# Two-block transformer kernel: post-norm sums of squares added on VectorE, and both scan directions' scores in one block

## The reference

```
scores = einsum('bhtd,bhjd,bhtjd->bhtj', qi, ki, decay)      # j <= t forward, j >= t backward
o_intra = einsum('bhtj,bhje->bhte', scores, vi)
o = rms_norm(o_f + rev(o_b), gn) * silu(cg)
```

```
x = x + rms_norm_2(mix, mix_post_g[l])
x = x + rms_norm_2(memory_cross_attention(...), mem_post_g[l])
x = x + rms_norm_2(conv_ffn_2(...), ffn_post_g[l])
```

## Time and profile before

| | |
|---|---|
| Median of 3 runs | 3217.31 us (3217.26 to 3220.99) |
| The profiled execution: time | 3217.78 us |
| The profiled execution: span from the first to the last instruction | 3216.0 us |
| Mean granted TensorE clock | 0.963 of full speed |
| TensorE matmuls busy | 2983.4 us, 93% |
| VectorE busy | 1520.6 us, 47% |
| ScalarE busy | 1281.8 us, 40% |
| GpSimd busy | 327.6 us, 10% |
| DMA | 254.09 MB, 79 GB/s in the mean |

### The profile page before, as it was taken

How to read it: one execution, slowest core, us unless ns; L and a number is a source line. 1 busy time by engine, 2 the same in 40 slices (tenths; PEclk the granted TensorE clock), 3 DMA queues, 4 the chain that set the end, 5 groups by cost and what they waited for, 6 DMA issues and landing times. The chain is left out here.

```text
span 3216.0 us, 39342 instructions
## 1 busy us (share of the span) xinstructions
PE 2983.4 (93%) x14872; PEld 2330.9 (72%) x14872; DVE 1520.6 (47%) x2141; ACT 1281.8 (40%) x1866; POOL 327.6 (10%) x285
## 2 busy tenths in 40 slices
PE   6989897899989999899899989999899899899998
PEld 2879775678768888576577768887675577678885
DVE  3346346555544442356643354442465563354432
ACT  3751334532233332434553343333434653433333
POOL 0010003500001100003000111100104001011100
PEclk8999999999999999999799999999999899999999
DMA  6100210045422222120022112222120131122222
GB/s 230 66 27 1 73 66 1 2 133 177 161 74 96 91 104 92 62 79 14 27 105 92 53 66 95 101 101 79 67 79 1 49 123 53 53 92 94 103 101 79
DMA packets 43556, 254.09 MB, mean 79 GB/s; under 512 B 4608, under 2 KB 6784, under 8 KB 15872
## 3 DMA queue, kind: packets, MB, share of 16 engines
q1 hardware_dynamic: 43392, 251.87, 21.9%
HBM read 249.75 MB, written 2.10 MB: 78 GB/s over the span
## 5 line engine op out<-in xcount | busy, mean ns | idle before, releaser
L238 DVE TENSOR_TENSOR ring_lo<-ring,ring_hi 128x2048 fp32r<-128x2048 f32 x201 | 460.7, 2292 | 881.5 <-ACT ring_hi L231 881.5
L289 PE MATMUL bank<-h_hi,ring_hi 128*128 128x512 f32 x1360 | 557.2, 410 | 17.2 <-DVE mix_lo L1588 6.4
L231 ACT ACTIVATE ring_hi<-ring 128x2048 fp32r<-128x2048 f32 x201 | 383.8, 1910 | 463.2 <-PE bank L289 343.3
L289 PE MATMUL bank<-h_hi,ring_lo 128*128 128x512 f32 x1360 | 534.1, 393 | 0.0
L1402 PE MATMUL bank<-h_hi,ring_hi 128*128 128x512 f32 x960 | 374.1, 390 | 5.7 <-DVE ring_lo L238 5.7
L1405 PE MATMUL bank<-h_lo,ring_hi 128*128 128x512 f32 x960 | 373.5, 389 | 0.0
L1406 PE MATMUL bank<-h_hi,ring_lo 128*128 128x512 f32 x960 | 373.5, 389 | 0.0
L289 PEld LDWEIGHTS bank<-h_hi,ring_hi 128*128 128x128 f32 x1360 | 257.2, 189 | 86.3 <-issue 22.1
L289 PEld LDWEIGHTS bank<-h_hi,ring_lo 128*128 128x128 f32 x1360 | 257.0, 189 | 60.0
L289 PE MATMUL bank<-h_lo,ring_hi 128*128 128x512 f32 x624 | 243.8, 391 | 0.0
L1402 PEld LDWEIGHTS bank<-h_hi,ring_hi 128*128 128x128 f32 x960 | 180.2, 188 | 45.3 <-issue 5.5
(11 more groups left out here) (449 smaller groups left out, 5089.0 us busy)
## 6 DMA issues: line engine op xcount, KB each, us to landing
ring<-in_stream SPq DMA_DIRECT2D x209, 1024.0 KB, 4.8
mod_w<-in_stream SPq DMA_DIRECT2D x64, 256.0 KB, 4.8
xT<-in_xT SPq DMA_DIRECT2D x2, 2048.0 KB, 14.8
const<-in_const SPq DMA_DIRECT2D x1, 2306.5 KB, 16.0
par<-in_par SPq DMA_DIRECT2D x3, 696.0 KB, 3.9
memT<-in_memT SPq DMA_DIRECT2D x2, 1024.0 KB, 4.9
out<-xT SPq DMA_DIRECT2D x1, 2048.0 KB, 6.3
ctxT<-in_ctxT SPq DMA_DIRECT2D x1, 1024.0 KB, 4.8
```

Of the source, the lines that this page charges most:

```text
L231: nc.scalar.activation(self.slab_hi(slab + j), self.slab(slab + j), ACT.Copy).then_inc(slab_rounded, 1)
L238: nc.vector.tensor_tensor(lower, self.slab(slab + j), self.slab_hi(slab + j).bitcast(F32), ALU.subtract)\
L289: ins = nc.tensor.matmul(out, lhsT, rhs, start=start and w is w_hi and x is x_hi, stop=stop and w is w_lo)
```

## The change

Post-norms: square 0 goes to a buffer of its own, which VectorE uses as a running total. VectorE adds the squares of tiles 1 to 6 to it, one add behind each tile in its list. TensorE multiplies the total by the ones and then the square of tile 7, so two products instead of eight. The wait for a free square buffer is now on VectorE's adds.

```
             def square(self, act, n):
                 act.wait_ge(self.sum_done.sem, self.sum_done.at(n + 1))
                 if n >= SQUARES:
-                    act.wait_ge(self.square_summed.sem, self.square_summed.at(n - SQUARES + 1))
-                nc.scalar.activation(self.squares[:, n % SQUARES, :], bank[:, n, :], ACT.Square).then_inc(self.square_ready.sem, 1)
+                    act.wait_ge(self.squares_added.sem, self.squares_added.at(n - SQUARES + 1))
+                nc.scalar.activation(self.square_place(n), bank[:, n, :], ACT.Square).then_inc(self.square_ready.sem, 1)
+
+            def add_square(self, dve, n):
+                if 1 <= n < KT - 1:
+                    dve.drain()
+                    dve.wait_ge(self.square_ready.sem, self.square_ready.at(n + 1))
+                    nc.vector.tensor_tensor(self.square_place(0), self.square_place(0), self.square_place(n), ALU.add)\
+                        .then_inc(self.squares_added.sem, 1)
 
             def sum(self, pe, n):
-                if n == 0:
+                if n == KT - 2:
                     pe.wait_ge(self.first_out.sem, self.first_out.at(1))
-                pe.wait_ge(self.square_ready.sem, self.square_ready.at(n + 1))
-                nc.tensor.matmul(bank[:, 0, :], con("ones"), self.squares[:, n % SQUARES, :], start=n == 0, stop=n == KT - 1)\
-                    .then_inc(self.square_summed.sem, 1)
+                    pe.wait_ge(self.squares_added.sem, self.squares_added.at(KT - 2))
+                    nc.tensor.matmul(bank[:, 0, :], con("ones"), self.square_place(0), start=True, stop=False)
+                if n == KT - 1:
+                    pe.wait_ge(self.square_ready.sem, self.square_ready.at(KT))
+                    nc.tensor.matmul(bank[:, 0, :], con("ones"), self.square_place(KT - 1), start=False, stop=True)\
+                        .then_inc(self.square_summed.sem, 1)
```

```
-            def scores_of(d, l):
-                return bank[:, 2 + 2 * d + l % 2, 0:256]
+            def scores_of(l):
+                return bank[:, 2 + l % 2, :]
...
                     for b in range(TB):
-                        last = nc.tensor.matmul(scores_of(d, l)[:, b * 64:(b + 1) * 64].rearrange("p (n m) -> p n m", m=m),
+                        last = nc.tensor.matmul(split(scores_of(l)[:, b * P:(b + 1) * P], m)[:, :, t_half[d], :],
...
-                        last = nc.tensor.matmul(split(O(h)[:, b * P:(b + 1) * P], m)[:, :, t_half[d], :], v[:, CB + b, h, :],
-                                                masked[:, d, l % 2, b * 64:(b + 1) * 64].rearrange("p (n m) -> p n m", m=m),
+                        last = nc.tensor.matmul(O(h)[:, b * P:(b + 1) * P], v[:, CB + b, h, :], masked[:, l % 2, b * P:(b + 1) * P],
                                                 start=False, stop=False, skip_group_check=True)
...
-                        intra(h, l, 0)
-                        intra(h, l, 1)
+                        intra(h, l)
...
-                            mask(h, l, 0)
-                            mask(h, l, 1)
+                            mask(h, l)
...
-                    for g in range(64 // m):
+                    for d in range(DIRS):
+                        act.wait_ge(level_done[d].sem, level_done[d].at(h * LEVELS + l + 1))
+                    act.wait_ge(intra_done.sem, intra_done.at(h * LEVELS + l - 1))
+                    for g in range(P // m):
...
             def rows_scaled(pool):
+                both = con("levels", LEVELS * P)
+                nc.gpsimd.tensor_tensor(both, both, con("levels", LEVELS * P, (LEVELS + 1) * P), ALU.add)
```

More of the change, by code:

```diff
@@ L738, in __init__, with square_place @@
                 self.next_scale_ready = Signal("next_scale_ready", 1)
+            def square_place(self, n):
+                return self.squares[:, 1 + (n - 1) % (SQUARES - 1) if n else 0, :]
             def square(self, act, n):
@@ L1526, in vector @@
                     post.read_first(dve)
+                    for n in range(KT):
+                        post.add_square(dve, n)
                     post.vector(dve, (at_down + FT * KT) // SLAB + 1)
@@ L1904, in scan_branch @@
             level_done = [Signal(f"level_done{d}", LEVELS * H) for d in range(DIRS)]
-            masked_by_dve = [Signal(f"masked_by_dve{d}", BY_DVE * H) for d in range(DIRS)]
-            masked_by_act = [Signal(f"masked_by_act{d}", (LEVELS - BY_DVE) * H) for d in range(DIRS)]
-            intra_done = [Signal(f"intra_done{d}", LEVELS * H) for d in range(DIRS)]
+            masked_by_dve = Signal("masked_by_dve0", BY_DVE * H)
+            masked_by_act = Signal("masked_by_act0", (LEVELS - BY_DVE) * H)
+            intra_done = Signal("intra_done0", LEVELS * H)
             keys_turned = [Signal(f"keys_turned{d}", H) for d in range(DIRS)]
@@ L2064, in merge, with mask @@
                     nc.vector.tensor_tensor(decay(h, d, l + 1), whole[:, :, 0, 0], whole[:, :, 1, 0], ALU.mult)
-                def mask(h, l, d):
-                    m = 1 << l
+                def mask(h, l):
                     if l >= 2 or h > 0:
[L2069 to L2074, removed]
+                        dve.wait_ge(intra_done.sem, intra_done.at(h * LEVELS + (l - 1 if l >= 2 else 0)))
+                    ones = con("levels", P, (LEVELS - 1 - l) * P).rearrange("p (o n) -> p o n", o=1).to_broadcast([P, TB, P])
+                    nc.vector.tensor_tensor(masked[:, l % 2, :].rearrange("p (b n) -> p b n", n=P),
+                                            scores_of(l).rearrange("p (b n) -> p b n", n=P), ones, ALU.mult)\
+                        .then_inc(masked_by_dve.sem, 1)
                 def recur(h, d):
@@ L2112, in turned_out, with mask @@
                                          ACT.Copy).then_inc(keys_out[d].sem, 1)
-                def mask(h, l, d):
+                def mask(h, l):
                     m = 1 << l
-                    act.wait_ge(level_done[d].sem, level_done[d].at(h * LEVELS + l + 1))
-                    act.wait_ge(intra_done[d].sem, intra_done[d].at(h * LEVELS + l - 1))
-                    for g in range(64 // m):
-                        out = masked[:, d, l % 2, :].rearrange("p (b n m) -> p b n m", b=TB, m=m)[:, :, g, :]
-                        ones = con("levels", 1, (d * (LEVELS + 1) + LEVELS - 1 - l) * P + (2 * g + t_half[d]) * m)
-                        last = nc.scalar.activation(out, scores_of(d, l).rearrange("p (b n m) -> p b n m", b=TB, m=m)[:, :, g, :],
+                    for d in range(DIRS):
+                        act.wait_ge(level_done[d].sem, level_done[d].at(h * LEVELS + l + 1))
+                    act.wait_ge(intra_done.sem, intra_done.at(h * LEVELS + l - 1))
+                    for g in range(P // m):
+                        out = masked[:, l % 2, :].rearrange("p (b n m) -> p b n m", b=TB, m=m)[:, :, g, :]
+                        ones = con("levels", 1, (LEVELS - 1 - l) * P + g * m)
+                        last = nc.scalar.activation(out, scores_of(l).rearrange("p (b n m) -> p b n m", b=TB, m=m)[:, :, g, :],
                                                     ACT.Copy, scale=ones)
-                    last.then_inc(masked_by_act[d].sem, 1)
+                    last.then_inc(masked_by_act.sem, 1)
                 def read_head(h):
@@ L2433, in build_program @@
                                               for m in range(2))
-            work["masked"] = ring_spare[:, 2 * size:2 * size + 1024].rearrange("p (d u n) -> p d u n", d=2, u=2)
+            work["masked"] = ring_spare[:, 2 * size:2 * size + 1024].rearrange("p (u n) -> p u n", u=2)
             work["diag"] = in_x[:, C_HEADS * ALLT:C_HEADS * ALLT + T]
```

30 lines of the change are left out of this document (14 added, 16 removed).

## The result

The changed kernel takes 3167.05 us in the median of 4 runs (3160.97 to 3173.60), the one before 3217.28 us; the ratio is 0.9845, with an interval of 0.9833 to 0.9856. The forecast was 3171.5 us, in a range of 3163 to 3182. Two things are to be explained: that it came out 4 us lower, and that the changed kernel's runs lie up to 13 us apart, where the runs shown of before were within 0.2 us but for one.

A forecast was written before the change was run, and what follows sets the result against it. TensorE, busy 93% of the span, was taken to bound the kernel. Scan 17.6 us plus post-norms 28.4 us made 46.0 us off 3217.8 us, 3171.8, put at 3171.5 us; range 3163 to 3182.

The forecast's parts named there:

- What bounds the kernel: Whole kernel: TensorE is busy 93% of the span, so shortening its stream shortens the kernel if other engines keep up.
- Scan, 17.6 us: Scan: 56 fewer TensorE instructions a head at 0.112 us, less waits; 5.1 us from the first head, 4.15 from each later.
- three waits: Scan head, TensorE waiting: 0.8 and 0.1 us behind level 0's updates, 0.7 before level 6's scores, 1.24 plus 0.4 at last `intra`.
- The clock rival: Scan: new TensorE waits lower the clock, 0.09 us more an instruction; slower than before, 3237 us with three later heads; 3%.
- The list's three items: Scan: the places where new TensorE waits arise (behind level 0, behind level 3, at last `intra`), together 2.1 us a head.
- The walk: Scan: three engines' instruction lists stepped through one head with trace durations; 34.6 us a head before, 30.4 after, 127.3 in all.
- Mix, 5.1 us: `mix_and_memory` post-norms, two: five sums saved ahead, 4.3 us, and 0.8 behind as key tiles follow sooner; 5.1 us each.
- Memory output, 4.9 us: `project` post-norms, two: 4.3 us from five sums, 0.6 more behind, where the logarithm waits for ScalarE's table load; 4.9 each.
- FFN, 4.2 us: `ffn` post-norms, two: VectorE's adds become the bound, TensorE waits 1.1 us; 4.2 us each, 3.2 to 4.9 by add time.
- six adds of 0.69 us with a drain, 0.77 us each: `ffn` post-norm: VectorE's adds behind its copy, priced at the copy's duration plus a drain, so the total comes at 2240.6.
- Post-norms, 28.4 us: All six post-norms: two each of 4.9, 5.1 and 4.2 us; bounds 24 to 30.6 us.
- POOL's joint mask at nothing: Ahead of the scan: one POOL mask instruction of 896 columns, about 1.7 us, costs zero, at most 1.7 us and covered.

The follow-up runs named there:

- again: The changed kernel repeated unaltered, to see its spread; 3170.15 us median of 5 runs, 0.9844 of the kernel before.
- again_2: The changed kernel repeated unaltered once more, beside a kernel with three further edits on the same chip; 3165.48 us median of 5 runs, 0.9848 of the kernel before.

## Why the prediction was right, point by point

- **What bounds the kernel** was right: in the scan and the post-norms what was taken off TensorE came off the time, less the waits that are named below.
- **Scan, 17.6 us: measured 18.9.** By heads: the first gave 5.55 us (5.1 forecast), the two in the middle 4.33 and 4.34 (4.15), the last with the scan's end 4.7. The price of an instruction, 0.11 us at 64 and at 128 columns, held, and so did the three waits: 0.71, 0.57 and 1.61 us idle, against 0.8 + 0.1, 0.7 and 1.24 + 0.4 = 1.64 (the rival on the clock says 1.9 for the last). The list's three items add up to 2.0 us and not to 2.1; measured, a middle head gave back 56 x 0.112 - 4.34 = 1.9. The walk was 0.5 us a head too slow, as it had already been 0.35 too slow for the kernel before.
- **Mix, 5.1 us: measured 4.98**, in two pieces, 4.30 ahead of the logarithm and 0.68 behind it, as the two terms had it (4.3 and 0.8). The squares of the memory's output stand 5.54 to 5.63 us apart, as foreseen.
- **Memory output, 4.9 us: measured 4.89.** The logarithm waits for the table load, 0.11 us longer than for the product.
- **FFN, 4.2 us: measured 3.19.** The mechanism was right and the size off: the step "six adds of 0.69 us with a drain, 0.77 us each" put the gap at 0.08 us, and the adds that also wait for a square stand 0.855 us apart; nor did the prediction reckon that the first add would come 0.54 us behind the copy. The first makes 0.4 us, the second, over the 0.08 us of a drain, some 0.5. That the lower end of its range, 3.2 us, was met is luck: it was priced with adds of 0.95 us each.
- **Post-norms, 28.4 us: measured 26.1; total, 46.0 us: measured 45.0** in the stretches that hold the change. The two errors partly cancel.
- **POOL's joint mask at nothing** held, though it takes 2.08 us and not 1.7: the scan starts at 209.0 to 212.0 us in the eight traces that have the new mask and no delay, against 212.7. It is not the mask that makes the start earlier: of the 2.7 us in the changed kernel 1.8 stand already at 50 us, where ScalarE's last instruction on `mod_rows` starts (50.07 us, 51.84 before), and the mask starts at 51.97.
- **The clock rival** was named for the wrong place. Inside the scan's heads the clock stayed at 1.00, as two rows of the changed kernel show (stretches of about a head each):

```profile
257.50:287.00 29.50, 27.18 (x238) 26.61 (x238) 21.79 (x59) 5.84 (x17) 0.00 (x0) 1.00 0.01 1
287.00:316.00 29.00, 26.84 (x236) 26.26 (x235) 21.44 (x58) 5.84 (x17) 0.00 (x0) 1.00 0.00 1
```

  Where it did act is in the attention stages, and at the scan's end as before the change. The rule quoted from the Trainium skill ("TensorE: Matmul & The Clock Gate", "Part 1: The HAM clock gate"), that activity lifts a slow default, is borne out in part only: the clock fell behind a wait of 2.78 us, and waits of 0.6 to 1.6 us in the scan did not bring it on; but it then stood at 0.50 for 24 us in which the profile shows TensorE busy throughout.
- **The median** of 3167.05 against the forecast's 3171.5 is partly luck. The prediction lacked a term for the other stretches: over the 45.0 us of the stretches the difference of the medians is 50.2 us here, 46.8 with `again` and 52.0 with `again_2`, and the changed kernel's own runs reach from 3156.85 to 3173.69. Whether a part of the rest belongs to the change stays open. The first layer's mix stage, up to its first square, takes 311.5 to 312.6 us in all nine traces with the new scan and 313.6 to 314.0 in the three without, with the same instructions; no experiment separates the place of that stage in time from anything else.

## What to carry to other kernels

Price a small float32 product by its weight loads, if the trace shows them to set the pace: where products of 64 and 128 columns stand equally far apart, joining two into one of double width halves their cost. When work is taken off the busiest engine, walk the lists of the others with the trace's own distances, since what comes back as waits (here 1.9 us a head) can be within reach of the order of a list: two moves of one instruction each took 7.7 us off the scan here, a part of it from a wait that the kernel before had too. And judge small edits by stretches cut at the same instructions in two traces, not by medians alone, and take more than one trace of each: two traces of the same kernel differed by 4.9 us in a stage that no edit touched.

## What the hardware showed that I had not expected

- One kernel, unaltered, ran the same stretch of 1479 instructions of TensorE in 300.9 or in 296.0 us, at a mean clock of 0.91 or 0.94: the clock stood at its lower level for about 27 us in one trace and for about 10 in the other (read in steps of 3 us), behind the same wait and with TensorE busy. Four instructions of it take 2.08 us at the lower level and 1.13 at the higher. The changed kernel spreads over 16 us in the five runs of `again`, whose times go with the mean granted clock, 0.969 to 0.960. The kernel before spreads over 5.6 us in 15 runs, and with 1.8 us more work at the scan's start over 11.7 us in 11; why the spreads differ is not shown.
- An add on VectorE of 0.69 us that depends on the one before it and on ScalarE costs 0.855 us behind a drain and 0.82 us behind a wait on the semaphore of the add before, in a row of six. Behind a copy out of PSUM the first add came 0.54 us later with a drain and at once without.
